# Dilated prompt attention takes its three groups in the order third, second, first

## The reference

```python
DIL_PATTERNS = ((128, 1), (512, 4), (2048, 16))      # (window, dilation) of the three head groups
def dilated_prompt_group(q, k, v, window, dilation):
    ...
    sc = jnp.einsum('bdnqhe,bdnkhe->bdnhqk', qb, kk).astype(jnp.float32) * (e ** -0.5)
    ...
    sc = jnp.where(mask[:, None], sc, -jnp.inf)
    m = jnp.max(sc, axis=-1, keepdims=True)
    ex = jnp.exp(sc - m)
    den = jnp.sum(ex, axis=-1, keepdims=True)
    o = jnp.einsum('bdnhqk,bdnkhe->bdnqhe', ex.astype(v.dtype), vv) / den.swapaxes(3, 4)
    lse = (m + jnp.log(den))[..., 0].swapaxes(3, 4)
def combine_groups(outs, lses):
    w = jax.nn.softmax(jnp.stack(lses, axis=0), axis=0)
    return jnp.sum(w[..., None] * jnp.stack(outs, axis=0).astype(jnp.float32), axis=0)
```

## Time and profile before

| what | us |
|---|---|
| median of 3 runs (lowest, highest) | 2599.3 (2593.54, 2603.27) |
| the profiled execution | 2600.69 |
| its span, first to last instruction | 2598.9 |

### The profile page before, as it was taken

How to read it: one execution, slowest core, us unless ns; L and a number is a source line. 1 busy time by engine, 2 the same in 40 slices (tenths; PEclk the granted TensorE clock), 3 DMA queues, 4 the chain that set the end, 5 groups by cost and what they waited for, 6 DMA issues and landing times. The chain is left out here.

```text
span 2598.9 us, 40492 instructions
## 1 busy us (share of the span) xinstructions
PE 2480.7 (95%) x16039; PEld 2354.4 (91%) x16039; DVE 1124.1 (43%) x1944; ACT 575.8 (22%) x1328; POOL 877.1 (34%) x444
## 2 busy tenths in 40 slices
PE   6899999999999999999999889799999999999996
PEld 6899999999999998999765567699899999999996
DVE  7532323223236864311566455765832232222226
ACT  5300000000014441211555344112410000000002
POOL 2233333333345542432000121344233333333332
PEclk9999999999999999999999898799999999999998
DMA  5122121222213332321211353551211211111111
GB/s 182 55 91 75 68 89 64 94 72 87 79 64 134 129 135 105 124 90 72 75 43 45 94 209 127 180 199 60 78 68 60 92 49 49 49 49 49 41 41 66
DMA packets 85311, 229.45 MB, mean 88 GB/s; under 512 B 8889, under 2 KB 47330, under 8 KB 84034
## 3 DMA queue, kind: packets, MB, share of 16 engines
q1 hardware_dynamic: 79066, 207.90, 23.1%
q10 hardware_dynamic: 6088, 19.23, 1.9%
HBM read 196.69 MB, written 74.39 MB: 104 GB/s over the span
## 5 line engine op out<-in xcount | busy, mean ns | idle before, releaser
L801 PE MATMUL ps<-u_hi,w_hi 128*128 128x352 f32 (+1 forms) x2880 | 930.7, 323 | 32.8 <-DVE w_lo L1853 15.1
L802 PE MATMUL ps<-u_lo,w_hi 128*128 128x352 f32 (+1 forms) x2880 | 922.5, 320 | 0.0
L803 PE MATMUL ps<-u_hi,w_lo 128*128 128x352 f32 (+1 forms) x2880 | 920.6, 320 | 0.0
L704 POOL TENSOR_TENSOR w_hi<-raw,zero 128x1024 fp32r<-128x1024 f32 x178 | 342.0, 1922 | 1306.1 <-PE ps L801 1132.7
L801 PEld LDWEIGHTS ps<-u_hi,w_hi 128*128 128x128 f32 x2880 | 543.8, 189 | 42.3 <-DVE w_lo L1853 15.4
L802 PEld LDWEIGHTS ps<-u_lo,w_hi 128*128 128x128 f32 x2880 | 544.1, 189 | 0.9
L803 PEld LDWEIGHTS ps<-u_hi,w_lo 128*128 128x128 f32 x2880 | 543.4, 189 | 0.0
L707 POOL TENSOR_TENSOR w_lo<-raw,w_hi 128x1024 fp32r<-128x1024 f32 x178 | 437.6, 2458 | 14.0
L1950 DVE SCALAR_TENSOR_TENSOR x<-ps,x 128x352 f32<-128x352 f32 (+1 forms) x528 | 270.9, 515 | 209.8 <-PE ps L803 209.6
L1941 DVE TENSOR_TENSOR h<-ps,silu 128x352 f32<-128x352 f32 (+1 forms) x120 | 62.0, 516 | 679.4 <-PE ps L803 679.3
L801 PE MATMUL ps<-h_hi,w_hi 128*128 128x352 f32 (+1 forms) x1056 | 341.3, 323 | 5.3 <-DVE x L1950 2.7
(11 more groups left out here) (290 smaller groups left out, 2669.5 us busy)
## 6 DMA issues: line engine op xcount, KB each, us to landing
raw<-in_wstream SPq DMA_DIRECT2D x186, 512.0 KB, 3.2
out_win_out<-in_cache_win SPq DMA_DIRECT2D x23, 1424.0 KB
latn<-in_cache_mla SPq DMA_DIRECT2D x128, 80.0 KB, 1.8
scratch_gates<-stage ACTq DMA_DIRECT2D x16, 516.0 KB, 2.6
out_win_out<-in_cache_win SPq DMA_DIRECT2D x7, 1168.0 KB
kv_d<-in_cache_win SPq DMA_DIRECT2D x24, 256.0 KB, 7.5
sgt<-scratch_gates SPq DMA_DIRECT2D x16, 352.0 KB, 3.8
scratch_x_mid<-x SPq DMA_DIRECT2D x1, 4128.0 KB, 13.1
```

What stands on the lines that cost most here:

```text
L704: nc.gpsimd.tensor_tensor(hi, raw[:, s % RAW], zero[:].to_broadcast([P, UW]), ALU.add).then_inc(w_hi_done, 1)
L801: a = mm(out, wh, xh, start=start, stop=False)
L802: mm(out, wh, xl, start=False, stop=False)
L803: return a, mm(out, wl, xh, start=False, stop=stop)
```

## The change

`GROUP_ORDER = (2, 1, 0)` replaces the ascending order in `GSTEPS`, and the places that named a group by its number name it by its place in the order: which group is loaded first, second, third, which group's records wait for how many stores, and what the first scores of a group wait for.

```diff
-        GSTEPS = [(g, n) for g in range(NG) for n in range(8)]
+        GROUP_ORDER = (2, 1, 0)
+        GSTEPS = [(g, n) for g in GROUP_ORDER for n in range(8)]
...
-            load_group(0)
+            load_group(GROUP_ORDER[0])
...
-                    load_group(1)
+                    load_group(GROUP_ORDER[1])
             def load_records(g):
                 for k in range(NREC):
-                    sp.wait_ge(rec_stored[k], 16 * (3 if g == 2 else 2))
+                    sp.wait_ge(rec_stored[k], 16 * (3 if g == GROUP_ORDER[2] else 2))
...
                 if s == 8:
-                    load_group(2)
+                    load_group(GROUP_ORDER[2])
...
-                    load_records(0)
-                    load_records(1)
+                    load_records(GROUP_ORDER[0])
+                    load_records(GROUP_ORDER[1])
...
-            load_records(2)
+            load_records(GROUP_ORDER[2])
...
                 if n == 0:
-                    pe.wait_ge(g_landed[g % 2], 48 * (g // 2 + 1))
+                    pe.wait_ge(g_landed[g % 2], 48 * (s // 16 + 1))
```

## The result

The changed kernel takes 2603.3 us (median of 12 runs, 2600.99 to 2605.64), the kernel before in the same comparison 2599.5 us (12 runs, 2592.56 to 2603.27): a ratio of 1.0022, 95% interval 1.0012 to 1.0032. The profiled execution took 2603.19 us.

A forecast was written before the change was run, and what follows sets the result against it. Prompt attention was taken as bound by full DMA engines, TensorE's pace and clock, with early steps chained to cached-row arrivals. Terms -5 + 9.5 + 1.2 - 3.5 = +2.2 us gave 2602 us, range 2594 to 2611 us.

The forecast's parts named there:

- Arrivals: First eight steps: GpSimd's last product within 1 us of 1555 us; VectorE waits 8 us or more for sequence 5.
- Steps 0 to 7: First eight steps: cheap steps stay held by cached-row arrivals, last reduction starts sooner; -5 us, bounds -8 and -1.6.
- The bound of -1.6 us: First eight steps: gain falls to 1.6 us if one further two-tile step is at half clock.
- Steps 8 to 15: Second group stays, with the sampled tokens' products beside it: 0 us.
- Steps 16 to 23: Last eight steps: exchange paid, 24.60 to 34.1 us, +9.5 us; VectorE's waits for GpSimd add +1.2 us.
- add-on: Last eight steps: VectorE's negations wait for GpSimd's splits, +1.2 us (0 to 4.7).
- The sign set for failure: Forecast fails if the clock in steps 17 to 23 is below 0.8, or if GpSimd's products move.
- The tail: After step 23: a shorter transfer queue brings the last records to the weighting sooner; -3.5 us, bounds 0 and -5.
- the bound of 2.8 us: After step 23: VectorE's fourth merge product ends 2.8 us before the records came, limiting the gain.
- Half clock in the moved steps: Steps 17 to 23: two-tile steps at half clock, 3.3 us each, 2624 us if all seven; chance 0.09.
- First eight steps win all: First eight steps: cache rows come sooner, 10.9 us won in full, sum -5.2 us, 2594 us; chance 0.06.
- Exchange paid in full: End pays, nothing won ahead, tail keeps its 8.46 us: +10.7 us, 2610 us; chance 0.13.

The follow-up runs named there:

- the last kernel above: Order first, third, second plus VectorE's reduction of sampled products two steps later, against the kernel before: 2592.0 us, ratio 0.9981.

## Why the prediction held, step by step

*Arrivals.* Right: GpSimd's last product at 1554.59 us (within 1 us of 1555). VectorE's wait for sequence 5 was 7.43 us, a little under the 8 or more that were forecast, since the cheap steps ahead of it took (1542.41 - 1529.38) / 4 = 3.26 us each and not 2.67: the pace was read from the third group, with no half clock and no products of GpSimd beside it. The wait hid that error.

*Steps 0 to 7, -5 us.* Measured -4.1 at the copy of step 7. The last reduction starts at 1558.19 us and not at 1556.96 as its product would allow, for two reasons on VectorE's and TensorE's timelines: negations held by GpSimd (1.19 and 0.44 us more than 0.17), which the term had left out, and the values at half clock behind the idle time (0.94 us more); together they are more than the 1.23 us, so part of them was hidden. The Trainium skill's page "SBUF — State Buffer" (section "SBUF: two separate sides") says that GpSimd's instructions and some of VectorE's (those in a two-port mode, and those with two inputs in SBUF against an instruction of GpSimd that reads SBUF) share a pair of ports, which the one that starts first holds for its whole instruction while the other is blocked. The trace agrees for negations, which end as GpSimd's products do, though no run shows in which mode they run; reductions are not held (0.94 us at 1554.11, into the product of 1554.59). The bound of -1.6 us, if the longer idle time cost a further step at half clock, was not reached: the clock came back by 1560.58 us, ahead of the two-tile steps.

*Steps 8 to 15, 0 us.* Measured -0.7: before, step 15 ran at a half clock (7.70 us between copies), after at 1.00 (6.63 us).

*Steps 16 to 23, +9.5 and +1.2 us.* Measured 36.33 - 24.60 = +11.7, 1.0 us more than their sum. The steps themselves were right: 4.65, 4.21, 4.26, 4.21 and 4.26 us between copies from step 17 to 21. The mis-sized part is its add-on: the waits for GpSimd came to 0.2 us (one negation, 0.36 us; the last one is over before the second pair of splits), and in their place the last two steps took 5.27 and 6.09 us at a clock of 0.64, 2.9 us over 4.22. This is the half clock: at 1.00, in the kernel with 76 small matmuls, the same two steps took 4.53 and 3.59 us. There no scores of a next step fill the waits for ScalarE, whose copies of the transposed probabilities end less than 0.1 us ahead of the values. The same drain stood in before (3.58 and 3.31 us instead of 2.67), so I had its rows and read them as a wait for GpSimd alone. The sign set for failure (a clock below 0.8 in steps 17 to 23) did not come over all seven, where it is 0.88. Step 16 was 3.38 us, not 4.5, since TensorE left step 15 at full clock.

*The tail, -3.5 us.* The weighting begins 11.15 us behind the last copy instead of 14.08: -2.9. What ends the wait is the merge product and not the records, as the bound of 2.8 us in the prediction had it. The store's wait in the queue shrank by 6.5 us (8.46 to 1.92), where 5.0 were forecast (8.46 us at 292 GB/s are 2.5 MB, and not the prediction's 2.6), so the records were not late. A further -1.8 us I had not seen: the first instruction of the weighting takes 0.18 instead of 1.96 us. Before, it stood under a split of GpSimd that ends at 1639.62 + 2.40 = 1642.02 us, and it ended at 1642.06.

*Sum.* Forecast +2.2 us; the traces' terms are -4.1 - 0.7 + 11.7 - 2.9 - 1.8 = +2.2 us at the weighting, and the spans differ by 2.5. The time, 2603.3 us, lies 1.3 us over the forecast. But every term was off by 0.6 to 1.8 us, and the misses (+0.9 - 0.7 + 1.0 + 0.6 - 1.8) cancel, so the closeness is in part luck. It holds for the traces: by the ratio of the timed runs the loss is 5.7 us, 2.6 times the forecast.

*The rivals.* Half clock in the moved steps: two of seven were hit, and it would have decided from four on. First eight steps win all: no; even with half of the cached rows left out they won 5.7 of 10.9 us, as GpSimd's products and half clock hold them. Exchange paid in full: the end paid 11.7 us, but what was won ahead and behind was there; with the reduction two steps later, where the start wins 1.1 us, the order costs 8.5 us.

*Open.* By timed runs the loss is nearer to 6 us than to 2.5 (ratios 1.0022 and 1.0023). The executions of before scatter over 2592 to 2606 us, those of the change over 2601 to 2606; the three traces of before are of 2600.65 to 2602.9 us, so what its executions near 2593 us do otherwise isn't shown. The runs on record give a lead: of 90 executions of before that ran beside the experiments (without one at a clock of 0.932) the 23 with a mean granted clock of 0.982 or 0.983 take 2595.5 us in the mean, the 27 with 0.979 or less 2600.6 us; all 24 of the change lie at 0.974 to 0.981. Time goes with the clock, then, and how often TensorE falls to half clock may be a good part of the loss. That it is the cause was not tested.

## What to carry to other kernels

A cheap step is worth only what the arrival leaves where a step is chained to one (here 4.1 of 10.9 us): before reordering, find the floor under the early place, the next floor behind it (here the record stores), and then lift the floor. Letting the consumer lag two steps behind the producer won 0.18%, where the reordering alone lost 0.22%. By the traces, dear work belongs where transfers are awaited or a queue drains (the timed runs don't show the gain), and the last steps of a pipeline should be priced from the rows of the last steps, not from the middle ones.

## What I had not expected of the hardware

An instruction of 0.17 us on VectorE (a 128x4 negation) takes up to 1.77 us (in the last kernel above) when a product of GpSimd is under way, and an addition of 128x32 1.96 us instead of 0.18; both end within 0.05 us of GpSimd's instruction. Through a shared buffer this locks two engines into one pace: 3.49 us a step with no transfer late. And half clock isn't only behind long waits: in the changed kernel it stands from 1526 to 1536 us (0.50), ahead of the wait of 8.48 us, and gaps of 1.56 and 0.73 us ahead of the values in the last two steps went with a clock of 0.64.
